# A two-block float32 model on one core: the second block's input projection by seven products of 256 tokens, with GpSimd and ScalarE in the work around it

## What is computed

```
x = x + 0.5 * swiglu(rms_norm(x, ffn1_norm), w_gate, w_up, w_down)      # hidden width 2816
h = rms_norm(x, mix_norm)
proj = h @ w_in                                                         # 1024 -> 3600
qkv_a, z_a, a_a, b_a, qkv_b = split(proj, [1536, 512, 8, 8, 1536])
o_a = gdn_mixer(...)     # short convolution of width 5 + silu on qkv_a, q and k l2-normalized, gated delta rule
o_b = dilated_mixer(...) # q and k rms-normalized per head, relative bias looked up by distance, softmax
x = x + concat(o_a, o_b) @ w_out
x = x + 0.5 * swiglu(rms_norm(x, ffn2_norm), ...)
x = rms_norm(x, final_norm)
```

## Time and profile before

| | us |
|---|---|
| median of 3 runs (lowest, highest) | 3377.99 (3375.49, 3378.41) |
| the profiled execution's own time | 3375.62 |
| its span in the profile | 3373.9 |
| first feed-forward of block 2 | 1983 to 2395 |
| projection, first to last of its 232 large matmuls | 2397.4 to 2615.5 |
| first logits of the attention | 2630.3 |
| second feed-forward | 2943 to 3353 |

### The profile page before, as it was taken

How to read it: one execution, slowest core, us unless ns; L and a number is a source line. 1 busy time by engine, 2 the same in 40 slices (tenths; PEclk the granted TensorE clock), 3 DMA queues, 4 the chain that set the end, 5 groups by cost and what they waited for, 6 DMA issues and landing times. The chain is left out here.

```text
span 3373.9 us, 72513 instructions
## 1 busy us (share of the span) xinstructions
PE 3131.4 (93%) x28246; PEld 2288.2 (68%) x28247; DVE 1942.7 (58%) x3735; ACT 867.9 (26%) x1539; POOL 334.0 (10%) x286
## 2 busy tenths in 40 slices
PE   8998999799989999999799969999999799999997
PEld 5445886577764447885577748888544477588886
DVE  1585664456651676662666576664548665566644
ACT  1116110356641134112466520000111622100000
POOL 1000000322230000002222320000000043000000
PEclk9999999799989999999899979999999999999999
DMA  7110323399942112223599812222362000122221
GB/s 281 63 63 14 125 88 150 120 355 378 379 177 79 63 38 88 87 89 150 222 371 378 324 66 88 87 84 91 85 146 89 12 3 3 63 75 88 88 92 71
DMA packets 83623, 447.89 MB, mean 133 GB/s; under 512 B 19904, under 2 KB 20040, under 8 KB 39632
## 3 DMA queue, kind: packets, MB, share of 16 engines
q1 hardware_dynamic: 55200, 377.51, 30.1%
q0 software_dynamic: 25280, 64.54, 6.1%
q10 hardware_dynamic: 2928, 3.07, 0.3%
HBM read 412.05 MB, written 32.89 MB: 132 GB/s over the span
## 5 line engine op out<-in xcount | busy, mean ns | idle before, releaser
L1139 PE MATMUL pb<-arena,streamed 128*128 128x256 f32 x1952 | 452.6, 385 | 20.5 <-DVE lnw L2371 10.8
L1139 PEld LDWEIGHTS pb<-arena,streamed 128*128 128x128 f32 x1952 | 376.9, 193 | 75.6 <-issue 21.6
L1019 PE MATMUL pb<-arena,xT 128*32 x3008 | 347.3, 274 | 18.8 <-issue 12.1
L713 PE MATMUL pb<-xT,streamed 128*128 128x512 f32 x832 | 363.9, 596 | 0.0
L1019 PE MATMUL pb<-streamed,xT 128*32 128x128 f32 x9024 | 350.5, 274 | 7.2 <-issue 7.2
L1019 PEld LDWEIGHTS pb<-arena,xT 128*32 128x32 f32 x3008 | 320.5, 110 | 32.0 <-issue 26.4
L1019 PEld LDWEIGHTS pb<-streamed,xT 128*32 128x32 f32 x9024 | 322.9, 110 | 10.8 <-issue 10.8
L713 PEld LDWEIGHTS pb<-xT,streamed 128*128 128x128 f32 x832 | 157.8, 191 | 196.7 <-issue 196.5
L1591 ACT ACTIVATE streamed<-arena 128x3072 f32 x94 | 260.2, 2768 | 56.4 <-SPq L476 37.8
L1139 PE MATMUL pb<-arena,am 128*128 128x256 f32 x976 | 227.3, 379 | 0.0
L713 PE MATMUL pb<-arena,streamed 128*128 128x512 f32 x464 | 204.4, 597 | 3.4 <-DVE xT L2419 3.3
(11 more groups left out here) (454 smaller groups left out, 4987.2 us busy)
## 6 DMA issues: line engine op xcount, KB each, us to landing
arena<-in_w_moe SPq DMA_DIRECT2D x192, 1024.0 KB, 9.2
streamed<-in_w_tail SPq DMA_DIRECT2D x87, 1024.0 KB, 5.0
streamed<-in_w_layer SPq DMA_DIRECT2D x78, 1024.0 KB, 4.9
xT<-xs_dram POOLq DMA_DIRECT2D x22, 512.0 KB, 8.6
ys_dram<-xT POOLq DMA_DIRECT2D x88, 128.0 KB, 9.1
xs_dram<-lnw POOLq DMA_DIRECT2D x12, 512.0 KB, 17.9
lnw<-in_ln_par POOLq DMA_DIRECT2D x4, 1024.0 KB, 6.4
rel_dram<-xtok POOLq DMA_DIRECT2D x1, 4092.0 KB, 87.0
```

The costliest lines, as they stand in the source:

```text
L713: last = mm(pb[bank][:, 0:cols], unit(w, u, k), rhs[:, k * cols:(k + 1) * cols], start=(k == 0), stop=(k == KC - 1))
L1019: last = mm(pb[m][r0:r0 + MOE_BLOCK, 0:FW], rows, w, start=(k == 0), stop=(k == KC - 1))
L1139: last = mm(pb[p][:, 0:HALF], stat(i), mov(i), start=(opens and i == 0), stop=(closes and i == steps - 1))
```

## The change

1. **Projection by seven products.** The 28 groups become 14 pairs, each of 28 matmuls by 256 tokens, two products to a bank: `pb[0]`, `pb[1]`, `pb[6]` whole and half of `pb[7]`. The order of the groups is q, k, attention q, attention k, v, then attention v, then z.
2. **GpSimd** makes the sums of the weight quarters of every pair (four `tensor_tensor` of 128 x 512) and multiplies each finished pair by `rs` (one of 128 x 1024). Its two DMAs for the bias are put in the same queue behind pairs 1 and 3.
3. **ScalarE** copies the first product out of PSUM for each pair and takes over the copy of the norm sums (L2492 before). The softplus and sigmoid of a and b are moved to g = 4.
4. **VectorE** reads the products out in seven operations of 128 x 256 per pair (`in_reads`, `in_upper`). The sums of the projection's inputs are made in the last parts of the feed-forward. The work on a and b moves to g = 3, 5, 6, the norms of the attention's k and q to g = 21 to 27.
5. **a and b** are projected first, by eight matmuls of 32 columns in four column groups of the array, into `pb[5]`. v is transposed at g = 25.
6. **Feed-forward, both.** `rms` on TensorE moves behind output pair 1; `add_square` and `row_scale` on VectorE move behind `recombine` of pairs 0 and 1.
7. `scale_rows` and its parameter load at the end of the last layer are left out (nothing reads their result), with VectorE's wait for them.

The core of the diff, first GpSimd's queue:

```diff
-                scale_rows(2 * l + 1)
+                if l + 1 < DEPTH:
+                    scale_rows(2 * l + 1)
...
-            pool.wait_ge(rel_copied, 2)
-            pool.dma_start(bass.AP(tensor=rel_dram, ...), rel_row...).then_inc(rel_stored, 16)
-            pool.wait_ge(rel_stored, 16)
-            pool.dma_start(cut(hank, 896), ...).then_inc(hank_loaded, 16)
+            def in_weights(c):
+                j = AB_SLOT + 1 + c
...
+                pool.wait_ge(w_loaded[j % SLOTS], (DEPTH * LAYER_USES + j // SLOTS + 1) * 16)
+                if c:
+                    alone(pool)
+                    pool.wait_ge(prod_ready, IN_PRODS + N_PROD * (c - 1) + 6)
+                add(s1, a21, a22, ALU.add)
+                pool.drain()
+                add(s2, s1, a11, ALU.subtract).then_inc(w_summed, 1)
+                add(a21, a11, a21, ALU.subtract)
+                pool.drain()
+                if c == 0:
+                    pool.wait_ge(sq_summed, 2)
+                add(s4, a12, s2, ALU.subtract).then_inc(w_summed, 1)
+            def scale_pair(c):
+                pool.wait_ge(prod_read, IN_READS + 4 * c + 4)
+                y = cut(in_pair(c), S)
+                nc.gpsimd.tensor_tensor(y, y, rs.unsqueeze(1).to_broadcast([P, 2, S]), ALU.mult).then_inc(lin_free, 2)
+            in_weights(0)
+            for c in range(IN_PAIRS):
+                if c + 1 < IN_PAIRS:
+                    in_weights(c + 1)
+                if c == 0:
+                    pool.wait_ge(ab_scaled, 1)
+                    alone(pool)
+                scale_pair(c)
+                if c == 1:
+                    pool.wait_ge(rel_copied, 2)
+                    pool.dma_start(bass.AP(tensor=rel_dram, ...), rel_row...).then_inc(rel_stored, 16)
+                if c == 3:
+                    pool.wait_ge(rel_stored, 16)
+                    pool.dma_start(cut(hank, 896), ...).then_inc(hank_loaded, 16)
```

TensorE, for each pair c (`at_group(g)` holds the small matmuls: g = 0 `rms`, 1 the bias lookup, 2 a and b turned, 4 to 19 one norm sum each, 25 the transposes of v):

```diff
-            for g in range(N_H):
-                linear(pair(34 + g // 2), g % 2, xns[1], ...)
+            for c in range(IN_PAIRS):
...
+                bank_free(0)
+                product(0, 0, a11, part(0, 0))
+                product(0, 1, a12, part(1, 0))
+                pe.wait_ge(w_summed, IN_SUMS + 2 * c + 1)
...
+                bank_free(1)
+                product(1, 0, s2, added(1))
+                pe.wait_ge(w_summed, IN_SUMS + 2 * c + 2)
...
+                product(1, 1, a21, added(2))
+                at_group(2 * c)
+                bank_free(2)
+                product(6, 0, s1, added(0))
+                product(6, 1, s4, part(1, 1))
...
+                product(7, 0, a22, added(3))
+                at_group(2 * c + 1)
```

VectorE (`in_upper` has four more operations of the kind of `in_reads`, from `pb[6]` and `pb[7]`):

```diff
+            def in_reads(c):
+                dve.wait_ge(first_copied, 2 * DEPTH * MIXED + c + 1)
...
+                v.tensor_tensor(out[:, 0:HALF], p1, pb[0][:, HALF:S], ALU.add).then_inc(prod_read, 1)
+                dve.wait_ge(prod_ready, IN_PRODS + N_PROD * c + 4)
+                v.tensor_tensor(u2, p1, pb[1][:, 0:HALF], ALU.add)
+                dve.drain()
+                v.tensor_tensor(u3, u2, pb[1][:, HALF:S], ALU.add).then_inc(prod_read, 1)
+            def in_upper(c):
...
-            for g in range(N_H):
-                dve.wait_ge(lin_ready, DEPTH * LIN_LAYER + g + 1)
-                v.tensor_tensor(grp(big, g), pb[g % 2][:], rs, ALU.mult).then_inc(lin_free, 1)
+            for g in range(2, N_H):
+                if g < H_AB:
+                    if g % 2 == 0:
+                        in_reads(g // 2)
+                    else:
+                        in_upper(g // 2)
...
+                if g - 2 < H_SQ or g in V_AT:
+                    dve.wait_ge(lin_free, DEPTH * LIN_LAYER + 2 * (g // 2) + 2)
+                    convolve(g - 2 if g - 2 < H_SQ else H_V + V_AT.index(g))
...
-                    v.tensor_scalar(grp(nrm, c % 8), pb[2 + c % 4][:], ...).then_inc(nsum_used, 1)
+                for c in K_NORM_AT[g] if g in K_NORM_AT else ():
+                    apply_norm(1, c)
+K_NORM_AT = {21: (0,), 22: (1,), 23: (2, 3), 24: (4,), 25: (5,), 26: (6,), 27: (7,)}
```

More of the change, by code:

```diff
@@ L71 @@
 FF_FIRST = [0, 53]
+AB_SLOT = 34
+H_SLOTS = [14, *range(10), 12, 13, 10, 11]
 assert LAYER_PAIRS % SLOTS == TAIL_PAIRS % SLOTS == 0
@@ L1176, in _ @@
             feed_forward(0)
-            pe.wait_ge(dn_free, KC)
-            for g in range(N_H):
-                linear(pair(34 + g // 2), g % 2, xns[1], DEPTH * LIN_LAYER + g, g % 2, norm=1 if g == 0 else None)
+            pe.wait_ge(prod_read, products_read(0, FF_SUMS))
+            alone(pe)
+            w = pair(AB_SLOT)
+            for k in range(KC):
+                r0 = k % 4 * 32
+                pe.wait_ge(xn_ready, KC + k + 1)
+                last = mm(pb[5][r0:r0 + 32, :], unit(w, 0, k)[:, r0:r0 + 32], grp(xns[1], k), start=(k < 4), stop=(k >= 4))
+                if k == 0:
+                    last.then_inc(slot_free, 1)
@@ L1180, in _, with at_group @@
+            last.then_inc(ab_made, 1)
+            def at_group(g):
                 if g == 0:
-                    rms(1)
+                    rms(1, 2)
                 if g == 2:
+                    pe.wait_ge(ab_scaled, 1)
+                    for n in range(NCH):
+                        for r in range(2):
+                            last = mm(pb[5][r * CH:(r + 1) * CH, n * 16:(n + 1) * 16], ab_out[:, n * CH:(n + 1) * CH],
+                                      sum16[:, :], start=True, stop=True)
+                    last.then_inc(ab_tr, 1)
+                if g == 6:
+                    pe.wait_ge(g_ready, 1)
+                    for r in range(2):
+                        h2 = slice(r * CH, (r + 1) * CH)
+                        last = mm(cut(pb[5][h2, 0:NCH * GH], GH), gtri[h2, :], cut(ga[h2, :], UN)[:, :, r * GH:(r + 1) * GH], start=True, stop=True)
+                    last.then_inc(gc_ready, 1)
+                if g == 1:
@@ L1201, in _ @@
[L1201 to L1209, removed]
-                last = mm(cut(pb[1][h2, 0:NCH * GH], GH), gtri[h2, :], cut(ga[h2, :], UN)[:, :, r * GH:(r + 1) * GH], start=True, stop=True)
@@ L1677, in _, with first_product @@
             feed_forward(0)
-            rms(1, dn_free, 0)
-            for g in range(N_H):
+            def first_product(c):
+                if c:
+                    act.wait_ge(prod_read, IN_READS + 4 * (c - 1) + 2)
+                    alone(act)
+                act.wait_ge(prod_ready, IN_PRODS + N_PROD * c + 2)
+                fn(in_first, pb[0][:, 0:HALF], ACT.Copy).then_inc(first_copied, 1)
+            rms(1, dn_free, 0, lambda: first_product(0))
+            for g in range(N_H):
+                if g % 2 == 0 and 0 < g < H_AB:
+                    first_product(g // 2)
+                if g == 4:
+                    act.wait_ge(ab_ready, 1)
+                    fn(gbeta[:, :], gbeta[:, :], ACT.Sigmoid)
+                    fn(ga[:, :], ga[:, :], ACT.Exp, scale=-1.0)
+                    act.drain()
+                    fn(ga[:, :], ga[:, :], ACT.Ln, bias=1.0)
+                    fn(alog[:, :], alog[:, :], ACT.Exp).then_inc(sp_ready, 1)
                 done = g - 2 if g - 2 < H_SQ else H_V + V_AT.index(g - 2) if g - 2 in V_AT else -1
@@ L2435, in _ @@
             input_sums(0)
-            for k in range(KC):
-                add_square(0, k)
-            dve.wait_ge(tok_done, 2 * DEPTH + 1)
             feed_forward(0)
-            row_scale(1)
             def convolve(g):
@@ new lines, in _ @@
+            v.tensor_tensor(sum16[:, :], identity[:, 0:16], identity[:, 32:48], ALU.add)
+            for c in (64, 96):
+                dve.drain()
+                v.tensor_tensor(sum16[:, :], sum16[:, :], identity[:, c:c + 16], ALU.add)
+            dve.drain()
+            in_reads(0)
+            dve.drain()
+            in_upper(0)
+            row_scale(1, 2)
+            dve.wait_ge(ab_made, 1)
+            v.tensor_tensor(ab_out, pb[5][:], rs, ALU.mult).then_inc(ab_scaled, 1)
+            dve.wait_ge(rel_ready, 1)
```

274 lines of the change are left out of this document (188 added, 86 removed).

## The result

Median 3432.87 us (3429.42 to 3440.77, 4 runs) against 3376.74 (3373.67 to 3378.41, 4 runs) for the kernel before: a ratio of 1.0171, 95% interval 1.0151 to 1.019. The forecast was 3398, its range ended at 3420: the direction was right, the size was not. The span grew by 56.6 us, from 3373.9 to 3430.5.

What follows compares the result with a forecast made beforehand. TensorE, busy 93% of the span, was taken as the bound, with VectorE close at the projection's end. 3375.6 less 21.4 (feed-forwards) plus 41 (projection) gave 3395, so 3398 for the median, range 3378 to 3420.

Steps and rivals of the forecast that it cites:

- part 3: GpSimd's queue in the projection: 7.7 us per pair; its bias DMA wait at c = 3 stalls TensorE 25 to 45 us.
- Part 1: Both feed-forwards: row scale behind pair 1's reads, fewer waits and no scale_rows, 21.4 us gained.
- Part 4: VectorE's projection tail: 80.8 us plus 6 of collisions with GpSimd, logits at 2671 instead of 2630.3, 41 us lost.
- the sentence on that rule: Convolution's first step in the tail: by the skill's port rule held as well, making the tail some 1 us longer.
- The stall hides them: Projection pairs 1 to 4: collisions make 16 to 18 us a pair, but the bias DMA stall covers them.
- B: Rival on the projection: DMA 95 us, GpSimd 8.5 a pair, pair 5 15 us later, tail 10 longer; 3422, chance 0.18.
- C: Rival, faster: at c = 3 the bias lands before it is missed, DMA under 55 us; 3367 or 3349, chance 0.10.

Runs made afterwards that it cites:

- e1: The changed kernel with GpSimd's two drains in each pair's weight sums replaced by a semaphore increment and wait; 3400.49 us, ratio 1.0083.
- e6: The kernel before with the feed-forward parts of the change alone, the projection as before; 3355.76 us, ratio 0.9943.
- e3: The changed kernel without GpSimd's drains in the weight sums and with the bias store's wait moved from after pair 3 to after pair 7; 3369.27 us, ratio 0.9978.
- e7: e3 with all of GpSimd's sums and scales in the projection cut to 8 columns of 512, semaphores kept; 3348.65 us, ratio 0.992.
- the probe: The kernel before with two GpSimd sums, a drain between them, put in right behind the issue of the bias store; 3372.01 us in one run.
- e2: The changed kernel, drains kept, with the bias store's wait and the lookup's DMA moved from after pair 3 to after pair 9; 3434.26 us, ratio 1.0171.
- e12: e3 with GpSimd's row scales alone cut to 8 columns of 512, its sums kept whole; 3363.82 us, ratio 0.9969.

## Why the prediction was wrong, point by point

**The step that failed** is in part 3: "4 x 1.25 + 2.35 + two drains = 7.7 us per pair", with the drains at next to nothing, and "behind it, at c = 3, stand the weight sums of pair 5". GpSimd did not reach the wait at c = 3. The drain inside pair 3's sums held it from 2436.7 to 2506.9. The price of a drain was right only where no DMA is in flight (0.14 us at pair 1). The hole was 66.4 us at pair 3 instead of 32.5 at pair 5. After against e1 that is 31.6 us of the stretch, of the 37 by which the span's growth (56.6) exceeded the forecast's 19.6 (41 less 21.4). The other 5.4 us are not traced one by one. The prediction listed what stands behind the new wait; the fault was to look only at instructions named waits. The trace of before held no drain on GpSimd behind a DMA in flight, so the price had to be bounded from both sides, and its upper bound was the DMA itself.

**Part 1** was right: 21.4 forecast, 20.3 by e6. In the trace of after the logits-to-end stretch is 7.6 shorter (9.5 forecast) and the start 6.4 earlier (3.9 forecast, but starts scatter by more than that between runs, see the table; TensorE's idle time just before the start fell from 8.83 to 4.99 us, by 3.8).

**Part 3's other sizes** were right. The DMA was issued at 2422.1; the forecast of 2437 was on a clock without part 1, 11.9 us later, so 2425. It took 84.6 us (forecast 80, range 70 to 95). An addition of 512 took 1.27 alone (forecast 1.25). The store's queue was busy for 43.8% of 16 engines from 2420 to 2510, so some 7 engines' worth: the Trainium skill (DMA: Bandwidth & Descriptors, Rules for kernel authors) confines a DMA with an outermost dimension of 8 to 8 engines. The trace is in line with it, though a mean share cannot show which engines worked. The forecast's 75 us had divided by 8 engines without saying so.

**Part 4** was right: the tail from group 18's read at 2605.56 to the last norm's end at 2694.2 took 88.7 us, forecast 86.8. Its collisions are 4.0 by experiment (e3: 2549.1 to 2636.9, 87.8; e7: 2524.8 to 2608.6, 83.8), forecast 6, and the tail without them 83.8, forecast 80.8: two small errors that partly cancel. TensorE waited 1.3 to 4.8 us for reads, five times; 3 to 6 each was said.

The one-input step of the convolution was counted as not held. It was: 1004 ns on average in e3, 486 in e7. The Trainium skill (GPSIMD Engine Reference, Key points) has VectorE's instructions in a 2-port mode contend with GpSimd. The traces agree in that these steps are held; that they run in such a mode no run here shows. In the tail it cost 1.0 us as the sentence on that rule worked out (0.49, 0.83, 1.11 and 0.49 in e3); over all twelve it cost 6.2.

**"The stall hides them"** (collisions in pairs 1 to 4) fits the kernel as it was changed, and is incomplete: once the hole is gone they come out. Of the 22.9 us between e3 and e7 only 4.0 lie in the tail; the rest lies ahead of it, where the prediction had priced them at nothing. From GpSimd's sums for pair 2 to those for pair 6 e3 takes 74.9 us and e7 61.5: 18.7 us a pair with collisions, against 16 to 18 forecast.

**Rivals.** The result is nearest to B (3422), but B's causes were not there: the DMA took 84.6 us, not 95, and GpSimd's additions 1.27, not 1.4. That nearness is luck. C, faster, put at 3367 if nothing waited long on the DMA: e3 measures 3369. Its condition (a DMA under 55 us) was not met in any run; a later wait and no drain led to nearly the same time.

## What to carry to other kernels

In these runs a drain on GpSimd was a wait for the DMAs that GpSimd had in flight: before such an engine gets a role in the inner loop, either take its long DMAs to another queue or order its own operations by a semaphore. Work moved to GpSimd costs VectorE time in operations with two SBUF inputs and in some with one, not in reciprocals or reads of PSUM: here 30.6 us for some 110 us of GpSimd. That price only shows once larger holes are gone. When a change bundles parts, run the part with the plain gain alone: the feed-forward half at 3355.76 equals all that was repaired in the other half (3360.61), with far less new in it. It has the lowest median, and the lowest ratio to the kernel before, of the versions that keep the computation whole, and both beat the kernel before and the changed one.

## What was not expected of the hardware

- GpSimd's drain waits for its own DMAs: 85.06 us in the probe (landing 86.6), 70.2 in the changed kernel (84.6), 2.75 for the lookup (12.7), 11.95 in e2. Each of these four ends within 0.3 us of the landing (15.3 us for the one in e2). Arithmetic without a drain passes: 0.0 us behind the issue.
- ScalarE's drain does not wait so: its squares ran 19 and 28 us after it had issued the same 4 MB.
- VectorE's one-input multiplication from SBUF, 0.49 us alone, is held by GpSimd's `tensor_tensor` like those with two inputs: on average 1.00 with sums and scales, 0.65 with sums alone. The work on a and b at g = 3 shows it on a small tile, in single instances:

```profile
L2722 DVE TENSOR_SCALAR ab<-ab 128x64 f32<-128x64 f32 x1 | 2.2, 2201 | 0.1
```

(e3, where GpSimd's multiplication of 1024 ran beside it from 2428.50 to 2430.85; 0.19 in e7 and, with the light scales alone, in e12.)

- TensorE's granted clock was 0.56 over the 70 us of the hole, so most of it at the lower of its two levels (1.2 and 2.4 GHz), and its first four matmuls behind it took twice their time:

```profile
2508.34 3.73 PE L1300 MATMUL pb<-arena,sin_t 128*128 128x256 f32 x8 [66.44 <-POOL sin_t L672]
```

Eight records take 1.89 elsewhere. Against a hole of 66 us that is small; the hole itself is the cost.
